# Router on scaled rows in fp32, with the norm's root and the shift applied behind the products

## The reference

```python
x = x + gate1[:, None, :] * (merged @ w_out[l])

h = modulate(rms_norm(x, norm_moe_g[l]), shift2, scale2)   # h * (1 + scale2) + shift2
x = x + gate2[:, None, :] * hierarchical_moe(h, ...)

# in hierarchical_moe, t = h as (tokens, 2048)
g_logits = (t @ w_group) + b_group            # 4 groups
e_logits = (t @ w_router) + b_router          # 32 experts, 8 of a group
# group by argmax, two experts in it by top_k, gates by softmax
hid = silu(t @ w1[e]) * (t @ w3[e]);  y = (hid * gate) @ w2[e]
```

## Time and profile before

| | us |
|---|---|
| median of 3 runs | 3102.91 |
| the three runs | 3093.43, 3102.91, 3103.35 |
| profiled execution | 3101.83 |
| its span in the trace | 3099.9 |

### The profile page before, as it was taken

How to read it: one execution, slowest core, us unless ns; L and a number is a source line. 1 busy time by engine, 2 the same in 40 slices (tenths; PEclk the granted TensorE clock), 3 DMA queues, 4 the chain that set the end, 5 groups by cost and what they waited for, 6 DMA issues and landing times.

```text
span 3099.9 us, 50499 instructions
## 1 busy us (share of the span) xinstructions
PE 2824.0 (91%) x19396; PEld 2388.2 (77%) x19396; DVE 1422.5 (46%) x2153; ACT 1196.8 (39%) x1457; POOL 1681.9 (54%) x1274
## 2 busy tenths in 40 slices
PE   6999979999998999668878879799999999999998
PEld 1688868999998989524334349699989999998998
DVE  1388855466354766512122224267713343315344
ACT  1333344444544433301111024566644456644343
POOL 0000048898776967000000017867689987779798
PEclk8899989999999999789999989899999999999999
DMA  9533348796434969199999943434445554445443
GB/s 392 219 115 118 129 151 289 257 320 222 162 136 170 349 228 353 36 415 399 389 406 381 399 170 134 176 138 143 151 153 188 188 180 158 154 150 190 153 175 136
DMA packets 107839, 679.67 MB, mean 219 GB/s; under 512 B 12608, under 2 KB 16448, under 8 KB 34240
## 3 DMA queue, kind: packets, MB, share of 16 engines
q1 hardware_dynamic: 83088, 602.97, 51.6%
q10 hardware_dynamic: 24624, 74.86, 6.9%
HBM read 770.05 MB, written 2.10 MB: 249 GB/s over the span
## 4 chain that ended last, share of the span: by engine, by line
PE 76%; DMA 11%; DVE 4%; ACT 4%; POOL 2%; issue 2%; SPq 1%; ACTq 0%; DVEq 0%; POOLq 0%
PE acc L590 47%; PE wk L590 10%; PE acc L663 10%; DMA ring<-in_moe 7%; PE acc L667 5%; POOL w_lo L572 2%; PE acc L676 2%; DMA stage<-in_ada 2%; DMA stage<-in_main 1%; ACT w_hi L1320 1%; DMA side_buf<-in_ada 1%; ACT L1320 1%; SPq L522 1%; ACT hb L1320 0%; DVE hb L1902 0%
## 5 line engine op out<-in xcount | busy, mean ns | idle before, releaser
L572 POOL TENSOR_TENSOR w_lo<-stage,w_hi 128x512 fp32r<-128x512 f32 x1268 | 1674.7, 1354 | 1362.0 <-ACT w_hi L1320 963.2
L1320 ACT ACTIVATE w_hi<-stage 128x2048 fp32r<-128x2048 f32 x317 | 604.3, 1909 | 107.9 <-DMA stage<-in_main 107.0
L590 PE MATMUL acc<-xhl,w_hi 128*128 128x256 f32 x4064 | 526.1, 288 | 23.3 <-DVE xhl L1902 11.6
L590 PEld LDWEIGHTS acc<-xhl,w_hi 128*128 128x128 f32 x4064 | 509.5, 196 | 26.5 <-DVE xhl L1902 7.6
L663 PE MATMUL acc<-xhl,w_hi 128*128 128x512 f32 x1536 | 369.2, 393 | 0.7 <-ACT w_hi L1320 0.7
L663 PEld LDWEIGHTS acc<-xhl,w_hi 128*128 128x128 f32 x1536 | 284.2, 190 | 56.2 <-issue 0.9
L590 PE MATMUL acc<-xhl,w_lo 128*128 128x256 f32 x2032 | 272.4, 288 | 2.0 <-POOL w_lo L572 2.0
L590 PEld LDWEIGHTS acc<-xhl,w_lo 128*128 128x128 f32 x2032 | 257.1, 194 | 5.4 <-issue 2.5
L590 PE MATMUL acc<-h,stage 128*128 128x256 f32 x1024 | 235.7, 386 | 2.9 <-ACT h L1320 2.9
L590 PEld LDWEIGHTS acc<-h,stage 128*128 128x128 f32 x1024 | 193.6, 192 | 40.6 <-issue 15.1
L667 PEld LDWEIGHTS acc<-xhl,w_lo 128*128 128x128 f32 x1536 | 196.8, 191 | 9.4 <-POOL w_lo L572 2.0
(11 more groups left out here) (486 smaller groups left out, 4065.8 us busy)
## 6 DMA issues: line engine op xcount, KB each, us to landing
stage<-in_main SPq DMA_DIRECT2D x317, 1024.0 KB, 4.8
ring<-in_moe SPq DMA_DIRECT2D x192, 1024.0 KB, 10.8
side_buf<-in_ada ACTq DMA_DIRECT2D x128, 512.0 KB, 6.3
over_lo<-in_moe ACTq DMA_DIRECT2D x48, 1024.0 KB
over_hi<-in_moe ACTq DMA_DIRECT2D x42, 1024.0 KB
stage<-in_ada SPq DMA_DIRECT2D x32, 1024.0 KB, 8.1
stage<-in_sb SPq DMA_DIRECT2D x32, 1024.0 KB, 4.7
x<-in_x ACTq DMA_DIRECT2D x1, 2048.0 KB, 13.0
```

Of the source, the lines that this page charges most:

```text
L572: last = pool.tensor_tensor(w_lo[:, k % 2, cs], stage[:, k, cs], w_hi[:, k, cs].bitcast(F32), ALU.subtract)
L590: return pe.matmul(o, w, r, start=start, stop=stop)
L1320: return act.activation(o, i, f, **kw)
```

## The change

ScalarE no longer copies the projection's result: VectorE adds the bank times gate1 to `x` in one operation (`add_scaled`). For each chunk of the projection ScalarE writes `xa`, which is `x` times the gain with the scale (a2), in fp32, and squares the same tile into `R["wsq"]` (`scaled_rows`); VectorE adds the squares up (`add_squares`).

The router's chunk is not rounded or split. TensorE multiplies it in fp32 straight from `stage`: `xa` is the stationary operand, 64 columns of the chunk move, so tokens come out on the partitions (32 products). The sums of squares for each token are two products of one column. The shift's part of the logits, the same for all tokens, is 16 products with a broadcast column of `mod` as the stationary operand, and the router's bias one more. VectorE forms the inverse root for each token as a column (128 x 2) and the logits as product times root plus bias.

The transposes read `xa`; ScalarE multiplies by the root while it empties them, once to fp32 (`xt32`) and once rounded (`xt_hi`), and GpSimd subtracts to `xt_lo`. The shift is added when the gathered rows are copied (`rows_in`). The `spin` products, `channel_sum(2)`, `affine_split(2)` and the transposes of the logits go; `side_columns(3)` comes after the third group of transposes; the modulation's last column set (`modulation(5)`) is formed behind the routing. `side_buf` for the last set has 4 pieces in place of 8, since `xa` takes half of its memory. The load of ring slot 1, the fourth load of the experts, waits for the router's product, and those behind it in SyncE's list with it.

```diff
-SIDE_BUFS = (2, 2, 4, 8)
+SIDE_BUFS = (2, 2, 4, 4)
...
+    xa = sb("xa", [P, DT, T], at=XH0)
...
+    xt32 = sb("xt32", [P, 2, D], at=D0 + 16384)
...
+    def xt_bank(i):
+
+        return (BASE["router"] + 1 + i % 3) % 4
...
+            elif i == 3:
+                sp.wait_ge(chunk_done, kv0)
...
-        each(pool, 4, BASE["kv"] - 4, low)
+        each(pool, 4, BASE["router"] - 4, low)
+        pool.wait_ge(hi_ready, BASE["router"] + 1)
+        pool.memset(vtmp[:, 11:12], 0.0).then_inc(lo_ready, 1)
+        for i in range(8):
+            cs = slice(i % 4 * 512, (i % 4 + 1) * 512)
+            pool.wait_ge(xt_h, i + 1)
+            pool.tensor_tensor(xt_lo[:, i // 4, cs], xt32[:, i // 4, cs], xt_hi[:, i // 4, cs].bitcast(F32),
+                               ALU.subtract).then_inc(xt_l, 1)
...
-        side_columns(3)
-        spin(30, BASE["router"])
-        channel_sum(2)
-        spin(20, BASE["router"])
...
-        wide(*slot(BASE["router"]), split=4)
...
+        k, q = slot(BASE["router"])
+        pe.wait_ge(load[k], (q + ADA_TURNS + SB_TURNS) * 16 + 16)
+        pe.wait_ge(evac_done, BASE["router"] - 3)
+        for t in range(DT):
+            pe.wait_ge(rms_affine_done, 16 + t + 1)
+            for h in range(2):
+                last = gm(acc[:, k, h * 64:(h + 1) * 64], xa[:, t, h * P:(h + 1) * P], stage[:, k, t * P:t * P + 64], t + h == 0)
+        pe.wait_ge(evac_done, BASE["router"])
+        pe.wait_ge(rms_sq, 2)
+        for h in range(2):
+            last = mm(acc[:, xt_bank(2), h:h + 1], rms_red[:, h * P:(h + 1) * P], ones[:, 0:1])
+        last.then_inc(rms_sum, 1)
+        pe.wait_ge(mod_ready, 4)
+        for t in range(DT):
+            gm(acc[:, k, 128:192], mod[:, 48 + t:49 + t].to_broadcast([P, P]), stage[:, k, t * P:t * P + 64])
+        gm(acc[:, k, 128:192], vec[0:64, VC["b_rt"]:VC["b_rt"] + 1].to_broadcast([64, P]), ident[0:64, 0:64],
+           stop=True).then_inc(chunk_done, 1)
         for i in range(8):
             h, q4 = i // 4, i % 4
-            if i >= 4:
-                pe.wait_ge(xt_h, i - 3)
-                pe.wait_ge(xt_l, i - 3)
+            if i == 3:
+                side_columns(3)
+            if i >= 3:
+                pe.wait_ge(xt_h, i - 2)
+            if i == 2:
+                pe.wait_ge(rms_var, 2)
...
+        pe.wait_ge(mod_ready, 7)
         pe.wait_ge(rt_d, PICK_AT)
...
+        def scaled_rows(t):
+
+            act.wait_ge(evac_done, BASE["wout"] + t + 1)
+            fn(xa[:, t, :], x[:, t, :], ACT.Identity, scale=a2[:, t:t + 1]).then_inc(rms_affine_done, 1)
+            if t >= 2:
+                act.wait_ge(vo_d, t - 1)
+            fn(wsq[:, t % 2, :], x[:, t, :], ACT.Square).then_inc(sq_done, 1)
...
+        act.wait_ge(rms_var, 2)
+        fn(rinv[:, 0:2], rinv[:, 0:2], ACT.Sqrt).then_inc(rms_sd, 1)
+        act.wait_ge(rms_inv, 2)
         for i in range(8):
             act.wait_ge(xt_done, i + 1)
...
+            fn(xt32[:, h, cs], acc[:, xt_bank(i), :], ACT.Identity, scale=rinv[:, h:h + 1])
+            fn(xt_hi[:, h, cs], acc[:, xt_bank(i), :], ACT.Identity, scale=rinv[:, h:h + 1]).then_inc(xt_h, 1)
+            if i == 2:
+                act.wait_ge(rt_d, 3)
+                fn(R["eg"][:], R["eg"][:], ACT.Exp).then_inc(rt_a, 1)
+            if i == 3:
+                act.wait_ge(rt_d, 19)
+                fn(R["ex"][:], R["ex"][:], ACT.Exp).then_inc(rt_a, 1)
...
-                fn(xg[:, :, t, :], o[:, 0:GROUP, :], ACT.Copy)
-                fn(xgo[:, :, t, :], o[:, GROUP:GROUP + TEAM, :], ACT.Copy).then_inc(xg_ready, 1)
+                shift = mod[:, 48 + t:49 + t]
+                fn(xg[:, :, t, :], o[:, 0:GROUP, :], ACT.Identity, bias=shift)
+                fn(xgo[:, :, t, :], o[:, GROUP:GROUP + TEAM, :], ACT.Identity, bias=shift).then_inc(xg_ready, 1)
...
+        def add_scaled(k, q, t):
+            dve.wait_ge(chunk_done, q * 4 + k + 1)
+            stt(x[:, t, :], acc[:, k, 0:T], mod[:, 32 + t:33 + t], x[:, t, :], MUL, ADD).then_inc(evac_done, 1)
...
+        def add_squares(t):
+
+            dve.wait_ge(sq_done, t + 1)
+            if t:
+                dve.wait_ge(vo_d, t)
+                ins = tt(rms_red[:], rms_red[:], wsq[:, t % 2, :], ADD)
+            else:
+                ins = cp(rms_red[:], wsq[:, 0, :])
+            ins.then_inc(vo_d if t < 15 else rms_sq, 1)
...
-        rms(2, x)
-        split_lo(hb, 4)
-        modulation(5)
+        k, q = slot(BASE["router"])
+        dve.wait_ge(rms_sum, 2)
+        ts(rinv[:, 0:2], acc[:, xt_bank(2), 0:2], 1.0 / D, MUL, EPS, ADD).then_inc(rms_var, 1)
+        dve.wait_ge(rms_sd, 2)
+        dve.reciprocal(rinv[:, 0:2], rinv[:, 0:2]).then_inc(rms_inv, 1)
+        dve.wait_ge(rms_inv, 2)
...
-        for i in range(8):
-            dve.wait_ge(xt_h, i + 1)
-            cs = slice((i % 4) * 512, (i % 4 + 1) * 512)
-            tt(xt_lo[:, i // 4, cs], acc[:, i % 4, :], xt_hi[:, i // 4, cs].bitcast(F32), SUB).then_inc(xt_l, 1)
...
+        cp(R["bias"][:], acc[:, k, 128:192]).then_inc(rt_d, 1)
         dve.wait_ge(rt_d, done.next())
+        for h in range(2):
+            ins = stt(L[:, h, :], acc[:, k, h * 64:(h + 1) * 64], rinv[:, h:h + 1], R["bias"][:], MUL, ADD)
+        ins.then_inc(evac_done, 1)
...
+        modulation(5)
         dve.wait_ge(pos_done, 1)
...
+        dve.wait_ge(xt_l, 8)
         pick_rows(0)
```

More of the change, by code:

```diff
@@ L1312, in _ @@
                 channel_sum(3)
-            wide(*slot(BASE["pgate"] + c), split=12 if c == 0 else None)
+            wide(*slot(BASE["pgate"] + c), split=8 if c == 0 else None)
     @block.scalar
@@ L1602, in _ @@
[L1602 to L1611 removed]
+            step(k, q, lambda: None, more)
```

99 lines of the change are left out of this document (45 added, 54 removed).

## The result

| | us |
|---|---|
| kernel before, median of 5 runs | 3097.17 (3092.63 to 3103.35) |
| changed kernel, median of 5 runs | 3073.43 (3072.19 to 3079.11) |
| ratio | 0.9921, 95% interval 0.990 to 0.994 |
| changed kernel, profiled execution | 3073.43, span 3071.6 |

3076 was forecast: right in the time and in the direction. The gain has three readings: 23.7 us between the medians of this table, 27.8 in a second set (four runs of the changed kernel, 3077.65, against 3105.41 for the kernel before; ratio 0.9906, 0.988 to 0.993), and 28.4 between the two profiled executions, which the forecast of 26.5 was summed on.

The account below looks back on a forecast made before the run. Nothing hides the stretch from projection's end to first gather: 72.3 us becomes 44.3, 28.0 less, minus 0.7 and 0.8 for biased passes, 26.5 net. 3101.83 - 26.5 = 3075.3, 3076 on the median's scale, range 3063 to 3088.

Parts of the forecast that it names:

- Up to the logits: From the last projection product to the first routing step: 13.1 us, with 64 fp32 router records at 0.115 each.
- The holds in the routing: Routing up to the count: 6.9 us as before plus 8.0 for eight VectorE steps held by GpSimd's subtractions.
- The Exp: ScalarE's Exp in the routing, now behind the fourth piece and a table load: no cost; without holds 1 to 2 us.
- Count 2.5 and places 10.4: Count 2.5 us and places up to the first gather 10.4 us, both unchanged; low clock keeps the count at 2.35.
- The memsets: GpSimd's two memsets of 3.52 us each beside the places: 3.4 us, the middle between bounds 0 and 7.0.
- The sum: Last projection product to first gather: 44.3 us against 72.3, 28.0 less.
- The gather: ScalarE's copies become passes with a bias: 0.7 us slower up to the first freed slot, 8 tiles x 0.09.
- Nothing in the projection; 12.9 us of ring loads hidden: Output projection costs nothing more; five expert loads wait for the router's product, 12.9 us, hidden by 19 us.
- Rival A: Clock falls to 1.2 GHz in the router's 64-column products: 102 records cost 0.115 more each, 11.7 us; 3088, chance 0.14.
- Rival B: VectorE is not held by GpSimd in routing and places: 11.4 us of holds go; 3064 us, chance 0.14.
- Rival C: Side buffer of 4 pieces starves the projection, from a landing of about 8 us; 3112 us, chance 0.04.
- Rival D: Time comes back in the experts' stretch, by another bound or ScalarE's bias passes; about 5 us stay; 3097, chance 0.05.

Follow-up runs that it names:

- xt_vector: Changed kernel with GpSimd's memsets behind the selection and all eight `xt_lo` subtractions on VectorE; first gather 35.74 us behind the last projection product.
- two_input: Changed kernel with the tensor-scalar step R_over <- R_cnt made a two-input step; first gather 41.23 us behind the last projection product.
- clock_kept: Changed kernel with memsets behind the selection and filler products where TensorE waits (4, 3 and 20); first gather 39.69 us behind the last projection product.
- fill_longer: Changed kernel with memsets behind the selection, last four `xt_lo` subtractions on VectorE, filler of 4 and 34 products; median 3065.53 us, ratio 0.989.
- no_bias: Changed kernel with gathered rows copied without the shift; 11.94 us from first gather to the end of the first 32 expert records.
- squares_after: Changed kernel with squares again one product and one reduction over all of `x` behind the projection; first gather 57.71 us behind the last projection product.
- memsets_late: Changed kernel with GpSimd's two memsets of the over buffers moved behind the selection; median 3073.8 us, ratio 0.990.
- changed_again: The changed kernel once more, unchanged, for comparison on the same chip; median 3077.65 us, ratio 0.9906.

## Why the prediction was right, and which terms were off

- *Up to the logits, 13.1:* 12.3. The 64 records took 7.09 us as the chain has them (0.111 each, 0.115 taken), shift and bias 4.00, the sums 0.39, and the last step to R_gmax 0.8.
- *The holds in the routing, 6.9 + 8.0:* 12.3 from R_gmax to the count's first product (1245.72 to 1258.03), so 5.4 of holds rather than 8.0. The mechanism was right, as xt_vector shows: 4 of the steps were held ahead of R_ex and only 2 behind it, for 0.87 each. In two_input and clock_kept, with the same instructions in the routing, 8 were held and the end of R_pick was 2.3 later: the number was right for that case. The Exp, put at no cost because held steps cover it, cost nothing; with the cover gone it cost 1.3 (forecast 1 to 2).
- *Count 2.5 and places 10.4:* 2.6 and 10.3. The count kept its 2.35, but not for the reason given: the one-column products were over at 1249.8 with the clock at 1.00, and it fell near 1254.5 (0.82 in the stretch from 1252 to 1256 us), in a wait of TensorE for ScalarE (2.54 us up to 1255.05). In fill_longer the clock was still 1.00, and the count's ten records took 1.3 us (1251.24 to 1252.54).
- *The memsets, 3.4:* 6.2. This is the term that was mis-sized. I took the middle between two bounds and supported it with the rule of the Trainium skill as if each memset would hold one step for its rest. The rule is right on the kinds of steps (two_input). What I missed: the first step on SBUF behind the count is a tensor-scalar step, and while VectorE stands in it, it cannot reach the two-input steps that would pass; and it did not come in between the two memsets, so the second held it in full.
- *The sum, 44.3:* 43.6. The errors of -0.8, -2.6 and +2.8 cancel: the sum is better than its terms.
- *The gather, 0.7 slower:* 0.96 slower up to the end of the first expert records (12.43 against 11.47), of which the bias is 0.4 to 0.5 (no_bias); the gather also ran at low clock for 4.2 us where it was 3.3 before.
- *Nothing in the projection; 12.9 us of ring loads hidden:* yes, 93.64 against 93.66, and the loads' share in 1260 to 1264 us is already 0.00, 13 us ahead of the gather.
- *Rival A, the clock in the narrow products:* did not happen; the clock was 1.00 from 1240 to 1253 us. Its price for a record was about right: in squares_after, where TensorE stood still first, it was 0.22 (0.23 taken). The comparison with the transposes, given against it, was wrong as a sum: they moved 128 / 0.123 = 1041 columns in a microsecond, the new records 64 / 0.115 = 557. So that the rival stayed away was not foreseen for a sound reason. The runs show that products ran at the low clock behind a standstill of 7.29 us (squares_after), and that narrow ones right behind the projection kept the high one. They do not show that a standstill is needed: in the kernel before, the clock fell in or right behind a run of one-column products while TensorE was busy all the time. In the changed kernel the same 32 records did not bring it down, and nothing measured here tells the two cases apart. In the kernel before (TensorE's timeline, and busy time by stretch behind the line of the earlier trace rows):

```profile
1110.40 4.10 PE L590 MATMUL wk<-ones,side_row 128*128 128x1 f32 x32
1114.37 6.63 PE L663 MATMUL acc<-xhl,w_hi 128*128 128x512 f32 x16
```

```profile
1116.00:1120.00 4.00, 4.00 (x10) 3.10 (x10) 0.07 (x1) 0.00 (x0) 0.04 (x1) 0.50 0.64 213
```

- *Rival B, no holds:* fell by the trace. *Rival C:* with 3 pieces it is still not reached. Its point of decision (a landing of 8 us) left out how much waiting of VectorE the banks absorb: at 26.5 us of it in the projection TensorE lost nothing. *Rival D:* not seen; -1.8 us in the experts' stretch, within the spread.

The profiled gain (28.4) holds +4.7 from ahead of the projection and -4.2 from behind the gather, both about what profiles of these kernels differ by in stretches that no edit touched (the last part, 1219.2, is the lowest of the 14).

## What to carry to other kernels

Find the stretch that nothing hides and sum it step by step from its own rows; then list what GpSimd does beside VectorE's short steps and look at each kind: a long GpSimd instruction in a chain of 0.2 us steps can cost up to its whole length (6.2 us for two memsets of 3.5), and moving it behind the chain is one changed wait, which cost nothing up to the end of the first expert records (12.2 us from the gather, 12.4 without the move). A part's worth depends on the rest: removing 11.5 us of VectorE brought 7.6 alone, where one-column products at the low clock still stood in front of the sum, and 14.1 on top of the rest, where its absence made TensorE stand still. Where runs of the same instructions spread over 10 us, compare marks inside the trace from the same origin, and not the totals.

## What the runs showed of the hardware

- A subtraction of GpSimd that reads SBUF (1.25 us) held tensor-scalar and two-input steps of VectorE on SBUF that began beside it until it ended, but no reduction (0.27 at 1249.53), no reciprocal (0.17 in squares_after) and no step with its other operand in PSUM (0.17 at 1257.80). A memset of 3.5 us held tensor-scalar steps and let two-input steps pass (0.19 to 0.23 in two_input).
- A held step sometimes waits for one GpSimd instruction and sometimes for the next as well: 6.42 us through two memsets in the changed kernel, but only to the end of the first (2.99) in memsets_late. The same routing held 6 steps in some runs (changed, changed_again, memsets_late, no_bias) and 8 in others (two_input, clock_kept). What decides it stays open.
- A run of filler products has no fixed length: 20 of them took 6.16 and 7.49 us, and 34 took 7.84, by the clock that they met.
- The granted clock fell to 0.50 with TensorE busy throughout in the kernel before (1112 to 1120 us, behind 32 one-column records), and did not fall behind the same 32 records at 1246.16 in the changed kernel until near 1254.5. What decides it stays open.
